# Two-layer attention block on one core: input stream in two transfers, and values and indexer heads issued two at a time in turn

## The reference, cut to what matters

```python
def dsa_mixer(x, w_in, w_out, cos, sin):            # stage A
    q, k, v, g, qi, wi, ki = jnp.split(x @ w_in, cuts, axis=-1)   # 16 heads of 64; qi: 8 heads of 64
    rel = jax.nn.relu(jnp.einsum('bqhd,bsd->bqhs', qib, ki) * IDX_DIM ** -0.5)
    score = jnp.einsum('bqhs,bqh->bqs', rel, wib)   # the indexer; the 64 best keys of each query are kept
    p = jax.nn.softmax(logits, axis=-1)             # 16 heads
    o = jnp.einsum('bhqk,bqkhd->bqhd', p, vs)
    return (o * jax.nn.silu(g)) @ w_out

def stick_breaking_mixer(x, w_in, w_out):           # stage B
    log_stick = lax.cumsum(log_one_minus, axis=3, reverse=True) - log_one_minus
    a = jnp.where(before, jnp.exp(jax.nn.log_sigmoid(z) + log_stick), 0.0)
    o = jnp.einsum('bhqs,bshd->bqhd', a, v)         # 16 heads
    return (o * jax.nn.silu(g)) @ w_out
```

## Time and profile before

| | |
|---|---|
| median of 3 runs | 1005.32 us (1005.24 to 1006.49) |
| the profiled execution's own time | 1006.38 us |
| its span in the profile | 1004.3 us |
| PE busy | 988.8 us (98% of the span), 6580 records |
| DVE busy | 682.7 us (68%) |
| ACT busy | 554.3 us (55%) |
| POOL busy | 203.1 us (20%) |
| chain that ended last, PE's share | 95% |
| granted TensorE clock | 0.998 of full speed |

### The profile page before, as it was taken

How to read it: one execution, slowest core, us unless ns; L and a number is a source line. 1 busy time by engine, 2 the same in 40 slices (tenths; PEclk the granted TensorE clock), 3 DMA queues, 4 the chain that set the end, 5 groups by cost and what they waited for, 6 DMA issues and landing times.

```text
span 1004.3 us, 16788 instructions
## 1 busy us (share of the span) xinstructions
PE 988.8 (98%) x6580; PEld 891.6 (89%) x6580; DVE 682.7 (68%) x1052; ACT 554.3 (55%) x852; POOL 203.1 (20%) x193
## 2 busy tenths in 40 slices
PE   8999999999999999999999999999999999999997
PEld 7779769998997998888889899999898989989985
DVE  4779775764556578566556778876678666667973
ACT  5446573555666466456455457654455545546652
POOL 0002023500143451002003004321034300302610
PEclk9999999999999999999999999999999999999999
DMA  9634515465431546525414555447555442455541
GB/s 355 229 131 140 203 43 209 168 224 195 168 127 42 202 150 245 174 96 202 175 74 168 209 184 191 160 180 295 191 203 215 163 168 85 173 204 174 169 161 42
DMA packets 25117, 172.90 MB, mean 172 GB/s; under 512 B 2784, under 2 KB 2912, under 8 KB 4704
## 3 DMA queue, kind: packets, MB, share of 16 engines
q1 hardware_dynamic: 23328, 160.66, 45.2%
q10 hardware_dynamic: 1728, 11.40, 2.9%
HBM read 166.81 MB, written 5.24 MB: 171 GB/s over the span
## 4 chain that ended last, share of the span: by engine, by line
PE 95%; ACT 2%; DMA 1%; DVE 1%; issue 0%; POOL 0%; SPq 0%; ACTq 0%; DVEq 0%
PE banks L493 39%; PE banks L581 16%; PE banks L499 13%; PE banks L501 7%; PE banks L491 5%; PE banks L643 4%; PE banks L743 2%; PE banks L697 1%; PE banks L725 1%; DMA raw<-w 1%; PE banks L745 1%; PE banks L819 1%; PE banks L708 1%; PE banks L923 1%; PE banks L887 1%; PE banks L910 1%
## 5 line engine op out<-in xcount | busy, mean ns | idle before, releaser
L1538 DVE TENSOR_TENSOR wl<-raw,wh 128x1024 fp32r<-128x1024 f32 x300 | 378.7, 1272 | 166.7 <-ACT wh L1044 165.2
L1044 ACT ACTIVATE wh<-raw 128x1024 fp32r<-128x1024 f32 x300 | 313.2, 1054 | 198.2 <-PE banks L493 85.0
L493 PE MATMUL banks<-xx,wh 128*128 128x256 f32 x1152 | 214.3, 285 | 0.0
L493 PE MATMUL banks<-yy,wh 128*128 128x256 f32 x1024 | 187.8, 285 | 0.0
L493 PEld LDWEIGHTS banks<-xx,wh 128*128 128x128 f32 x1152 | 181.5, 191 | 2.0 <-issue 1.0
L499 PE MATMUL banks<-xx,wh 128*128 128x512 f32 x496 | 175.5, 398 | 0.0
L493 PE MATMUL banks<-xx,wl 128*128 128x256 f32 x576 | 161.8, 283 | 0.0
L493 PEld LDWEIGHTS banks<-yy,wh 128*128 128x128 f32 x1024 | 160.5, 192 | 0.6 <-issue 0.3
L493 PE MATMUL banks<-yy,wl 128*128 128x256 f32 x512 | 138.7, 283 | 0.0
L501 PE MATMUL banks<-xx,wl 128*128 128x256 f32 x496 | 137.9, 278 | 0.0
L581 PE MATMUL banks<-wh,xx 128*128 128x512 f32 x352 | 113.1, 400 | 2.6 <-ACT wh L1044 2.3
(11 more groups left out here) (208 smaller groups left out, 1450.5 us busy)
## 6 DMA issues: line engine op xcount, KB each, us to landing
raw<-w SPq DMA_DIRECT2D x149, 1024.0 KB, 4.8
m_scratch<-yy ACTq DMA_DIRECT2D x2, 1024.0 KB, 5.9
k_scratch<-kt ACTq DMA_DIRECT2D x2, 1024.0 KB, 7.3
kt<-k_scratch ACTq DMA_DIRECT2D x2, 1024.0 KB, 5.4
yy<-m_scratch ACTq DMA_DIRECT2D x2, 1024.0 KB, 6.6
h<-xt SPq DMA_DIRECT2D x4, 256.0 KB, 6.9
raw<-w SPq DMA_DIRECT2D x2, 512.0 KB, 6.1
v<-memt ACTq DMA_DIRECT2D x1, 1024.0 KB, 7.7
```

What stands on the lines that cost most here:

```text
L493: return pe.matmul(b[:, j, :], weights, o_[:, kk, :], start=k0 + k == 0 and q == 0 and (j == 0 or not both_open), stop=k0 + k == KT * p.de ...
L1044: act.activation(wh[:, n % 2, j, :], raw[:, n % RAW_SLOTS, j, :], ACT.Copy).then_inc(hi_ready, 1)
L1538: dve.tensor_tensor(wl[:, n % 2, j, :], raw[:, n % RAW_SLOTS, j, :], wh[:, n % 2, j, :].bitcast(F32), ALU.subtract).then_inc(lo_ready, 1)
```

## The change

- The stream x comes in two transfers of 512 KB instead of four of 256 KB, each behind a half of the first weights. ScalarE and VectorE treat the first half of the weights ahead of x.
- The indexer's heads are issued in pairs by `indexer_heads`: the early product of both, then the late product of both. Four hooks replace eight, and the first pair stands where head 1 stood.
- Stage A: `value_pair` issues the values of two heads in turn, at every even step. The turned probabilities have four tiles instead of two (two of them in a part of `qz` that is free then).
- Stage B: `z_values` does the same for two heads, at every even step; `z_args` has four tiles.
- The number and the shapes of all instructions other than the transfers of x are as before.

```diff
+        fourth = [qz[:, 8 + 2 * i:10 + 2 * i, :].rearrange("p a b -> p (a b)") for i in range(2)]
+        def turned(name, a):
+            if name == "A":
+                return (wk(4), wk(5), fourth[0], fourth[1])[a % 4]
+            return wk(4 + a % 2)
...
         def z_args(a):
-            return (wk(8), wk(9), third[1])[a % 3]
+            return (wk(8), wk(9), third[1], fourth[0])[a % 4]
...
-            x_pair(0)
+            def x_half(i):
+                sp.dma_start(h[:, 4 * i:4 * i + 4, :], xt[:, 4 * i:4 * i + 4, :]).then_inc(x_in[i], 16)
             sp.dma_start(raw[:, 0, 0, :], w[0][:, 0, :]).then_inc(first_half, 16)
-            x_pair(1)
+            x_half(0)
             sp.dma_start(raw[:, 0, 1, :], w[0][:, 1, :]).then_inc(raw_full[0], 16)
-            x_pair(2)
-            x_pair(3)
+            x_half(1)
             load(1, 1)
...
+                def value_pair(a):
+                    pe.wait_ge(t_evac, u0 + a + 2)
+                    g = a // 2
+                    if g >= 2:
+                        pe.wait_ge(dve_evac, p.base + g - 1)
+                    b = bank[p.pair + g % 2]
+                    for late in range(2):
+                        for head in (a, a + 1):
+                            r, cols, pr = slice(HD * (head % 2), HD * (head % 2) + HD), slice(HD * head, HD * head + HD), turned(name, head)
+                            if late:
+                                pe.matmul(b[r, P:S], v[:, 1, cols], pr[:, S:S + P], start=False, stop=True).then_inc(o_full, 1)
+                            else:
+                                pe.matmul(b[r, 0:S], v[:, 0, cols], pr[:, 0:S], start=True, stop=False)
...
-                        values(t - sums)
+                        if t % 2 == 0:
+                            value_pair(t - sums - 1)
...
-                (1, 1, 1): then((indexer_head, 0)), (2, 0, 1): then((indexer_head, 1)), (2, 1, 0): then((turn_unit, 2)),
-                (2, 1, 1): then((indexer_head, 2)), (3, 0, 0): then((turn_unit, 3)), (3, 0, 1): then((indexer_head, 3)),
-                (3, 1, 1): then((indexer_head, 4))})
+                (2, 0, 1): then((indexer_heads, 0)), (2, 1, 0): then((turn_unit, 2)),
+                (3, 0, 0): then((turn_unit, 3)), (3, 0, 1): then((indexer_heads, 2))})
...
-                pe.matmul(b[r, 0:P], v[:, 0, cols], pr[:, 0:P], start=True, stop=True)
-                pe.matmul(b[r, P:S], v[:, 0, cols], pr[:, P:S], start=True, stop=False)
-                pe.matmul(b[r, P:S], v[:, 1, cols], pr[:, S:S + P], start=False, stop=True).then_inc(o_full, 1)
+                for part in range(3):
+                    for head in (a, a + 1):
...
-                if t >= 5:
-                    hooks[c, j, 2] = lambda t=t: z_values(t - 5)
+                if t >= 6 and t % 2 == 0:
+                    hooks[c, j, 2] = lambda t=t: z_values(t - 6)
```

More of the change, by code:

```diff
@@ L350, in build @@
         first_half = sem("first_half")
-        x_in = [sem(f"x_in{i}") for i in range(4)]
+        x_in = [sem(f"x_in{i}") for i in range(2)]
         const_in, kiw_in = sem("const_in"), sem("kiw_in")
@@ L743, in values @@
                         pe.matmul(o, v[:, 0, sl], wk(4 + a % 2)[:, 0:S], start=True, stop=False)
-                        late = slice(P, S) if name == "A" else slice(0, S)
-                        mm = pe.matmul(o[:, late], v[:, 1, sl], wk(4 + a % 2)[:, S:S + late.stop - late.start],
-                                       start=False, stop=True)
+                        mm = pe.matmul(o, v[:, 1, sl], wk(4 + a % 2)[:, S:2 * S], start=False, stop=True)
                     mm.then_inc(o_full, 1)
+                def value_pair(a):
[11 more added lines that the diff above has]
+                                pe.matmul(b[r, 0:S], v[:, 0, cols], pr[:, 0:S], start=True, stop=False)
                 turns, _, sums = depth(name)
@@ L814, in indexer_head @@
                     pe.wait_ge(wi_ready, 1)
-                if a >= 2:
-                    pe.wait_ge(rel_ready, a - 1)
-                r = slice(HD * (a % 2), HD * (a % 2) + HD)
+                else:
+                    pe.wait_ge(rel_ready, a)
                 for t in range(2):
-                    mm = pe.matmul(bank[4 + a % 2][:, NEAR[t]], qi[r, a // 2, t * P:t * P + P], ki[r, 0:S if t else P],
-                                   start=True, stop=True)
-                mm.then_inc(is_full, 1)
+                    for head in (a, a + 1):
+                        r = slice(HD * (head % 2), HD * (head % 2) + HD)
+                        mm = pe.matmul(bank[4 + head % 2][:, NEAR[t]], qi[r, a // 2, t * P:t * P + P], ki[r, 0:S if t else P],
+                                       start=True, stop=True)
+                        if t == 1:
+                            mm.then_inc(is_full, 1)
             def then(*calls):
@@ L916, in z_values @@
                     pe.wait_ge(act_evac, PH["vb"].end)
-                pe.wait_ge(z_prob, a + 1)
+                pe.wait_ge(z_prob, a + 2)
                 g = a // 2
-                if a % 2 == 0 and g >= 2:
+                if g >= 2:
                     pe.wait_ge(dve_evac, pb.base + g - 1)
-                r = slice(HD * (a % 2), HD * (a % 2) + HD)
-                b, pr, cols = bank[pb.pair + g % 2], z_args(a), slice(HD * a, HD * a + HD)
-                pe.matmul(b[r, 0:P], v[:, 0, cols], pr[:, 0:P], start=True, stop=True)
-                pe.matmul(b[r, P:S], v[:, 0, cols], pr[:, P:S], start=True, stop=False)
-                pe.matmul(b[r, P:S], v[:, 1, cols], pr[:, S:S + P], start=False, stop=True).then_inc(o_full, 1)
+                b = bank[pb.pair + g % 2]
+                for part in range(3):
+                    for head in (a, a + 1):
+                        r, cols, pr = slice(HD * (head % 2), HD * (head % 2) + HD), slice(HD * head, HD * head + HD), z_args(head)
+                        if part == 0:
+                            pe.matmul(b[r, 0:P], v[:, 0, cols], pr[:, 0:P], start=True, stop=True)
+                        elif part == 1:
+                            pe.matmul(b[r, P:S], v[:, 0, cols], pr[:, P:S], start=True, stop=False)
+                        else:
+                            pe.matmul(b[r, P:S], v[:, 1, cols], pr[:, S:S + P], start=False, stop=True).then_inc(o_full, 1)
             project_tokens("vb", xh, xl)
@@ L1147, in turned_out @@
                 act.wait_ge(t_full, UBASE[name] + a + 1)
-                if a >= 2:
-                    act.wait_ge(o_full, OBASE[name] + a - 1)
-                turned = 3 * P if name == "A" else 4 * P
-                act.activation(wk(4 + a % 2)[:, 0:turned], bank[6 + a % 2][:, 0:turned], ACT.Copy).then_inc(t_evac, 1)
+                if a >= turned_kept(name):
+                    act.wait_ge(o_full, OBASE[name] + a - turned_kept(name) + 1)
+                n = 3 * P if name == "A" else 4 * P
+                act.activation(turned(name, a)[:, 0:n], bank[6 + a % 2][:, 0:n], ACT.Copy).then_inc(t_evac, 1)
             def soft_attention(name, heads, high, lag, start=1):
@@ L1186, in units @@
                 return lambda c, t, b: rope_raw(u0 + 2 * c + t, t, b)
+            hi(0)
             act.wait_ge(x_in[0], 16)
             x_high(0, None)
[L1190 to L1191 removed]
             x_high(1, None)
             hi(1)
[L1194 to L1196 removed]
+            act.wait_ge(x_in[1], 16)
+            x_high(2, None)
+            x_high(3, None)
             hi(2)
```

28 lines of the change are left out of this document (11 added, 17 removed).

## The result

The changed kernel takes 995.56 us (median of 4 runs, 995.19 to 996.07) against 1005.38 (1005.24 to 1006.49) before: ratio 0.990, 95% interval 0.9883 to 0.9917. It is 9.8 us faster, where 12.6 were forecast. The profiled execution has an own time of 995.88 and a span of 993.3 us; that of before had 1006.38 and 1004.3.

What follows compares the result with a forecast made beforehand. TensorE, busy 98% of the span, was taken as the bound. Terms of -0.2, -4.2, -2.9, -3.0 and -2.3 sum to -12.6 us: 993.8 from the profiled 1006.38, given as 992.7; own range 990.3 to 995.0, stated 989.5 to 997.5.

Steps and rivals of the forecast that it cites:

- Two small products at once: On TensorE, two heads' products on different halves of rows or columns start together and cost what one head costs.
- column halves run one behind the other: Rival for the values: column halves do not overlap, only entry and hook costs are saved; -7.9 us, 997.4; chance 0.09.
- each change drains the array: Rival: each change of column half between heads costs TensorE time, up to 0.17 us, giving 1008.3; chance 0.04.
- The indexer, -4.2: Around the indexer, eight heads in eight hooks become four pairs, saving 4 x 1.04 us of TensorE; late conversions costed at nothing.
- taken back by late conversions: Rival for the indexer: ScalarE waits in its queue for a late pair, cancelling the gain; -8.4 us, 996.9; chance 0.07.
- Values in A, -2.9: In stage A's attention, pairs of values remove four 0.55 us DVE waits, less four 0.33 collisions; "oa" begins 2.9 us earlier.
- the collision: In A, VectorE's normalising would run into GpSimd's subtraction, costing 0.33 us per period of two heads.
- Values in B's hooks, -3.0: In "qkb", heads 0 to 5 become three pairs, each saving a hook of 0.99 us of TensorE.
- Values in B's loop, -2.3: B's loop, paced by ScalarE's exponentials and a closing chain, ends 2.3 us earlier; bounds -1.3 and -3.7.
- The start, -0.2: Fewer, larger transfers of x before the first projections gain 0.2 us; bounds -0.8 to +0.5.
- PE alone decides: Rival: VectorE and ScalarE keep up, so TensorE's full saving counts; -17.3 us, 988.0; chance 0.08.
- The sum of -9.9: Estimate from the Trainium skill page: each of sixteen pairs of values costs about 0.17 us more, giving -9.9 us in all.

Runs made afterwards that it cites:

- GpSimd's waits: Changed kernel with two waits added on GpSimd: its subtraction waits for VectorE's normalising in attention A and VectorE's sum in B; 994.07 us.

## Why the prediction was right, and where its size was off

The direction and the mechanism held, and 995.6 lies in the stated range of 989.5 to 997.5; the forecast was 2.9 us too low. It lies above the forecast's own range, which ended at 995.0: the stated one holds it only because it was drawn out towards the rivals, of which the indexer's was half true. The bounds that the prediction gives for its terms add up to 988.6 to 995.3; how 990.3 to 995.0 came of them it does not say.

- **Two small products at once: right.** A pair costs what a head costs, in scores and in values, and its two heads start within 0.01 us of each other. The rival that column halves run one behind the other (997.4) and the one that each change drains the array (1008.3) are out: pairs start together, and in the run with both heads on one half, where they cannot, a hook costs 0.65 us more.
- **The indexer, -4.2: this step failed, it gave -2.3.** "I cost that at nothing" was wrong by 1.9 us. I had looked at the slack of the conversions, which did last: PE never waits for `wl`, so the sign that the prediction named for a lost cover did not appear either. The removed hooks had been the cover of another chain, from a projection's end over ACT's copy and DVE's rotation to the turning; and one copy stood behind a relu. The rival "taken back by late conversions" was right that ACT would wait in its queue, wrong in what that would hold up, and too dear at 4.2.
- **Values in A, -2.9: right, -2.9 alone.** PE waits for DVE as foretold, DVE's four waits of 0.55 for scores are gone, "oa" begins at 149.13, and the price of the collision, taken at 0.33 a period, was 0.37 (its rows leave 0.52 of the subtraction, not the 0.55 that it says; in the event 0.58 was left).
- **Values in B's hooks, -3.0: right, -2.95.**
- **Values in B's loop, -2.3: -1.8.** The chain at the end was forecast with a DVE without collisions; two sums took 1.11 and 1.12. With GpSimd's waits 0.45 of the missing 0.5 comes back. The bound named such a collision.
- **The start, -0.2: not contradicted.** Alone it gave -0.2, which the runs cannot tell from none, though the two profiled executions said -1.09.
- **The rival that PE alone decides** fell, for the reason given: DVE sets A's rhythm.

The terms that were off make 1.9 + 0.5 = 2.4 of the 2.8 us between 12.6 and 9.8; the other 0.4 is the difference between the sum of the four parts' medians and the whole. The sum of -9.9 that the prediction sets beside its own, and did not go by, is near the measured -9.8 by luck: a pair of values cost no 0.17 more than a head (in a hook of B 1.24 to the second product behind it, against 1.23; at B's end 0.80, 315.81 to 316.61, against 0.79). What was missing was missing elsewhere.

## What to carry to other kernels

Before a piece of work is taken out of a full queue, ask what chain on other engines it was covering: whoever consumes their result next is now early, and waits. Here 1.9 of 4.2 us went that way. It came back in two halves: when the relus no longer stood ahead of work that TensorE needed, and when the turnings, which are the consumer, were moved six products on. And when an engine becomes the one that sets the rhythm, look at what it shares with an idle one: a wait on GpSimd, which had time, gave VectorE 0.37 us in each 3.16.

## What was not expected of the hardware

Products on different halves of the rows ran fully side by side although one head's stood wholly ahead of the other's in the program (eight records in 0.93 us either way). On halves of the columns the second head's start was 0.27 us late, two passes, and no more. What sets these two passes was not tried.
